# Attention on one core: in the last three token tiles one of five value products stays full f32 instead of two

## What is computed

```python
# 8 query heads in 2 groups, 64 wide; three branches, each with its own keys and values
s = einsum('bgrqd,bgnd->bgrqn', q, ck) * scale      # compressed: 63 keys
o_c = einsum('bgrqn,bgnd->bgrqd', masked_softmax(s), cv)
# selected blocks (top 16 of 16 blocks: all causal keys) -> o_s; window of 512 keys -> o_w
o = gates[..., 0:1] * o_c + gates[..., 1:2] * o_s + gates[..., 2:3] * o_w
```

## Time and profile before

| | us |
|---|---|
| median of 3 executions | 1704.76 (1704.27 to 1705.28) |
| the profiled execution | 1703.56 |
| its span | 1701.8 |
| TensorE, VectorE, ScalarE busy | 1640.0, 1022.6, 626.8 |
| units 10 to 14: from the swap of unit 9 to that of unit 14 | 607.10 to 726.91 |
| unit 15 | 726.91 to 744.03 |

### The profile page before, as it was taken

One profiled execution on the slowest core, in us unless ns is written; L12 is line 12 of the kernel. 1 busy time (PEld: TensorE's weight loads), 2 busy tenths in 40 slices (PEclk: granted clock), 3 DMA queues, 4 the chain that ended last, 5 costly groups with the idle time before them and its releaser, 6 DMA issues.

```text
span 1701.8 us, 22018 instructions
## 1 busy us (share of the span) xinstructions
PE 1640.0 (96%) x8157; PEld 1328.3 (78%) x8157; DVE 1022.6 (60%) x1871; ACT 626.8 (37%) x1173; POOL 77.9 (5%) x126
## 2 busy tenths in 40 slices
PE   8899999998789999999999999999999999999997
PEld 6688888888666776678888888888888888888885
DVE  6833556555699988864346555555655565556432
ACT  6214434344677777752222211221221122114221
POOL 0111221121000000000000000000000000000000
PEclk9899999998799999999999999999999999999999
DMA  5433233226000000060111111211121111122000
GB/s 197 130 100 117 94 105 105 85 81 202 25 23 17 13 14 1 1 235 0 54 59 48 63 37 37 64 48 37 37 74 37 37 51 60 37 75 100 25 38 37
DMA packets 48987, 110.60 MB, mean 65 GB/s; under 512 B 8848, under 2 KB 17040, under 8 KB 48912
## 3 DMA queue, kind: packets, MB, share of 16 engines
q1 hardware_dynamic: 41488, 85.47, 15.1%
q0 software_dynamic: 7424, 24.12, 4.2%
HBM read 89.65 MB, written 19.92 MB: 64 GB/s over the span
## 4 chain that ended last, share of the span: by engine, by line
PE 87%; DVE 5%; ACT 2%; issue 2%; DVEq 0%; POOLq 0%; POOL 0%; ACTq 0%
PE ps L1461 27%; PE ps L1115 14%; PE ps L1117 14%; PE ps L1116 14%; PE ps L1261 4%; PE ps L1377 3%; PE ps L1334 2%; PE ps L1340 2%; PE ps L1448 1%; PE ps L1379 1%; PE ps L1284 1%; PE ps L1120 1%; PE ps L1380 1%; PE ps L1342 1%; DVE nb L1867 1%
## 5 line engine op out<-in xcount | busy, mean ns | idle before, releaser
L2005 DVE TENSOR_TENSOR h<-h,ps 128x512 f32<-128x512 f32 x336 | 225.3, 686 | 148.8 <-PE ps L1117 147.8
L1461 PE MATMUL ps<-htl,wuh 128*128 128x512 f32 x672 | 209.7, 393 | 0.0
L1461 PE MATMUL ps<-hth,wuh 128*128 128x512 f32 x672 | 209.6, 393 | 0.0
L1461 PE MATMUL ps<-hth,wul 128*128 128x512 f32 x672 | 209.6, 393 | 0.0
L1115 PE MATMUL ps<-wh,xth 128*128 128x512 f32 (+1 forms) x448 | 186.8, 417 | 14.8 <-DVE wl L1595 13.2
L1117 PE MATMUL ps<-wh,xtl 128*128 128x512 f32 (+1 forms) x448 | 170.9, 381 | 0.0
L1116 PE MATMUL ps<-wl,xth 128*128 128x512 f32 (+1 forms) x448 | 170.4, 380 | 0.0
L1059 ACT ACTIVATE ffh<-ffa 128x1024 fp32r<-128x1024 f32 x22 | 23.3, 1060 | 369.8 <-DVE ffa L2032 369.8
L1461 PEld LDWEIGHTS ps<-hth,wuh 128*128 128x128 f32 x672 | 126.3, 188 | 29.3
L1461 PEld LDWEIGHTS ps<-hth,wul 128*128 128x128 f32 x672 | 126.2, 188 | 29.1
L1461 PEld LDWEIGHTS ps<-htl,wuh 128*128 128x128 f32 x672 | 126.3, 188 | 28.8
(11 more groups left out here) (270 smaller groups left out, 3151.8 us busy)
## 6 DMA issues: line engine op xcount, KB each, us to landing
wuraw<-in_w_up SPq DMA_DIRECT2D x44, 512.0 KB, 5.1
wraw<-in_w_in SPq DMA_DIRECT2D x48, 256.0 KB, 3.3
proj_d<-stage POOLq DMA_DIRECT2D x48, 256.0 KB, 2.4
wdraw<-in_w_down SPq DMA_DIRECT2D x22, 512.0 KB, 3.6
rin<-proj_d POOLq DMA_DIRECT2D x32, 256.0 KB, 4.2
xraw<-in_xt SPq DMA_DIRECT2D x16, 256.0 KB, 5.8
owraw<-in_w_out SPq DMA_DIRECT2D x8, 512.0 KB, 5.6
h<-in_x SPq DMA_DIRECT2D x1, 4096.0 KB, 15.6
```

The source lines that it names most:

```text
L1461: mm = nc.tensor.matmul(ps[:, 2 * part + half, :], w_, x_[:, k, half * 512:(half + 1) * 512], start=(k == 0 and i == 0), stop=(k == NK - 1 ...
L2005: nc.vector.tensor_tensor(hh, hh, ps[:, 4 + o_ % 4, :], ALU.add).then_inc(dn_add, 1)
```

## The change

The rule for which tiles stay whole changes. Up to now tiles j with j % 5 of 0 or 2 are whole in every unit. Now this holds for units 0 to 9 only; in units 10 to 15 (t = 5, 6, 7) only those with j % 5 == 0 are whole, and those with j % 5 == 2 are split. `place_of`, `freed_by` and the semaphore counts follow from `whole`.

```diff
-            return st[0] == "turn_p" and st[2] % 5 in (0, 2)
+            return st[0] == "turn_p" and st[2] % 5 in ((0, 2) if st[1] // G < 5 else (0,))
```

## The result

The changed kernel takes 1710.92 us (median of 6 executions, 1710.35 to 1711.13) against 1704.51 (1703.89 to 1705.28): ratio 1.004, 95% interval 1.003 to 1.005, or 6.4 us more. That is inside the range on record, but not the likeliest case of the forecast (+2.4 us): it is the side of rival 3, which had a chance of 0.37.

A forecast was written before the change was run, and what follows sets the result against it. TensorE was taken to bound the stage, VectorE close behind; VectorE's work and waits made +3.0 us in units 10 to 14, unit 15 -0.6: net +2.4, a median of 1707.2 us, range 1700.5 to 1712.

The forecast's parts named there:

- likeliest case of the forecast: Whole kernel: VectorE's added work and waits use up TensorE's saving; between -3.4 and +3.4 us, net +2.4, chance 0.45.
- rival 3: Units 10 to 14: blocked copies decide, each of five holding VectorE 1.6 us; +9.6 us, about 1714; chance 0.37.
- five places: Tile 8 of units 10, 11; 4, 9 of 13; 4 of 14: copies wait across scores; 5.5 us of VectorE idle time.
- I take 1.1: VectorE's idle time charged for each copy blocked across a slot's scores: 1.1 us, between 0 and 1.6.
- a late VectorE: From unit 11 on VectorE was found late, so a blocked copy was priced at 1.1 us instead of 1.6.
- The sum: VectorE's busy time, subtractions and waits in units 10 to 14: 122.8 against 119.8 us; with unit 15, net +2.4.
- second, smaller wait: First slot of units 10, 12, 14: VectorE idles before tile 2's new subtraction; 3 x 0.7 = 2.1 us.
- -0.6: Unit 15: 1.2 us saved on TensorE less 0.6 lost, so 0.6 us shorter.
- Three runs ... lose some 0.2 each: Unit 15: three runs of three or four split tiles lose some 0.2 us each, 0.6 in all.
- Rival 2: TensorE stays the bound, VectorE's slack takes the subtractions; up to -6.4 us, 1698.4; chance 0.18.
- its own sign: What would show the blocked copies deciding: unit 13 alone grows by 3 us.
- half of the cost hidden: Lower end of the range: TensorE stays the bound with about half the cost hidden; about 1700.5 us.

The follow-up runs named there:

- e1: The changed kernel with a third place for turned tiles' high and low parts, the retention input cut to one buffer; 1700.99 us, 0.9977 of the kernel before.
- e4: The changed kernel without the 16 new subtractions, both matmuls of those products reading the high part; 1709.42 us, 1.0027 of the kernel before.
- e6: The kernel before with only five of the 16 tiles split: 7 of units 10, 11; 2, 7 of 13; 2 of 14; 1708.88 us, 1.0025.
- e5: The kernel before with 11 of the 16 tiles split, no copy blocked with scores in between; 1704.64 us, 0.9998.
- e9: The kernel before with only five tiles split: 2 of unit 10; 2, 7, 12 of unit 12; 12 of unit 13; 1702.81 us, 0.9991.
- e3: The kernel before, products unchanged, plus one VectorE subtraction of constants for each of the 16 tiles, its result unused; 1704.48 us, 0.9996.
- e7: The kernel before with only tiles 2, 7, 12 of unit 15 split; 1705.24 us, 1.0007 of the kernel before.
- e12: e1 with tile 12 of unit 15 kept whole; 1700.80 us, 0.9975 of the kernel before.
- e10: The changed kernel with each product in units 10 to 15 put ahead of the turn two tiles after it; 1717.67 us, 1.0074.
- e11: e1 with all tiles of units 10 to 14 split, and tiles 2 and 7 of unit 15; 1706.12 us, 1.0015 of the kernel before.
- e8: e1 with only j % 5 == 0 whole in all 16 units, 30 products split instead of 16; 1700.09 us, 0.9971.

## Why the prediction was right, and where it was not

- **What it had right.** The range (1700.5 to 1712), and the wait: copies of tiles 3, 4, 8, 9 and 13 held by products behind their own turns, the exponentials held behind them on ScalarE, and the five places where a slot's scores lie in between. All three show in the profile after, and e1, e4 and e6 show that they carry the loss. The counts came out (100, 98 and 98), so did 10.5 us of VectorE's waits for pth ("not below 7"). Unit 11 is 1.02 longer ("about 1"), unit 13, with two places, 1.62. The saving of 0.40 per product holds: unit 10 with one product changed is 0.40 and 0.41 us shorter in e5 and e9, unit 12 with three 1.11.
- **The price of a place, mis-sized.** "I take 1.1": e6 gives 1.28 to 1.42, mean 1.34 over the five (with a second blocked copy beside each), 1.2 us more in all. The reduction from 1.6 for "a late VectorE" was too large: the exponential takes the other way, through ScalarE to TensorE's next scores, and units that left VectorE 1.7 us and 4 us pay the same. In the trace the exponential went at 716.31, behind a copy that had been blocked for 1.47 us. The Trainium skill, "TensorE: Matmul & The Clock Gate", section "Architectural detail: the array is 16× 32×32, not 1× 128×128", states that ScalarE takes its instructions strictly in order, and this trace agrees.
- **The step that failed: "The sum" takes VectorE as the engine that bounds.** It came to 122.8 us where 123.6 was measured, but from terms that are not there. The 7.9 us of subtractions raised VectorE's busy time by 5.98 only; they cost 0.12 by themselves (e3), and 1.05 where the copies are blocked (e4 against the changed kernel). The "second, smaller wait" of tile 2, 2.1 us, costs nothing: unit 10 with only tile 2 split is shorter by its full 0.40 (e5, e9). In their place stands TensorE's own idle time, 11.2 us against 4.7 before, with the 5.3 us for exponentials in it, and the end of unit 14, 0.53 us longer although a product there saves 0.40; the sum had that place at nothing. That the sum was near is luck; the forecast's VectorE share "over 90%" came out at 89.9%.
- **Unit 15, wrong in sign.** "-0.6" stands against +0.81 at full clock (e7) and +2.03 in the changed kernel. "Three runs ... lose some 0.2 each": three waits took 0.37, 0.25 and 0.38, and the sum left out that the last run ends the unit. Nothing is left there to put into the time of a copy and a subtraction, and this one place lost 1.16 us. The clock, 1.22 us more, was in no term.
- **The rivals.** Rival 2 (TensorE stays the bound) described what happens without the blocked copies: e1 is at -3.6 us. Rival 3 is what came, well short of its full price (+3.8 in units 10 to 14, where it had +9.6), and not by its own sign, which had unit 13 grow by 3 us. The lower bound had no working: "half of the cost hidden" is put at 1700.5, but half of the forecast's cost of 8.8 us beside a saving of 6.4 gives 1702.8.

Still open is why the clock falls at the start of unit 15 in some kernels. The median is 6.4 us up, the units that hold the change 5.8 in the profile, of which 1.2 goes with the clock.

## What to carry to other kernels

When a tile moves from one ring of buffers to another, list for each producer which consumer frees its place, and where that consumer stands in the order of the engine that both wait on: a buffer that is freed by an instruction behind its own producer's input makes a wait of everything in between. One more place, found by halving a buffer that had time to spare, turned this change from 6.4 us slower into 3.6 us faster (0.9977). And an engine that is 88% busy is not near its bound by that: here VectorE took 6.7 us more at a cost of 0.12 and was the bound at 98%; what an added instruction costs is told by the chain that it joins, not by the share. At the end of a sequence nothing covers the last element: the ends of units 14 and 15 show it.

## What was not expected of the hardware

In the changed kernel, e1, e4 and e12 the granted clock was at half, 1.2 GHz, for about 3.4 us at the start of unit 15; in the changed kernel twelve transposes took 2.80 us from 733.51 where they take 1.53 at full clock. There it comes after two microseconds in which TensorE was busy 0.38 and 0.49. e10 (at 681 and 709) and e11 (at 708) fell inside units 13 and 14 in the same way; TensorE was busy 0.42 and 0.06 of the two microseconds from 706 in e11. But in the kernel before TensorE stood wholly idle from 727 to 728 and the clock stayed:

```profile
726.00:727.00 1.00, 0.79 (x3) 0.29 (x2) 0.97 (x5) 0.52 (x5) 0.00 (x0) 1.00 0.49 178
727.00:728.00 1.00, 0.00 (x0) 0.00 (x0) 0.96 (x3) 0.67 (x2) 0.00 (x0) 1.00 1.14 363
728.00:729.00 1.00, 0.99 (x9) 0.99 (x10) 0.70 (x2) 0.25 (x1) 0.00 (x0) 1.00 0.94 367
```

And e1 and e8, whose products are split alike from unit 10 on, differ: 17.55 us with the fall, 16.73 without, although TensorE was busy 0.62 and 0.19 of the two microseconds from 723 in e1, and 0.73 and 0.02 in e8. So the instructions of these units and the idle time just before don't decide it alone; the runs don't say what does.
